# Reordering the attention heads of the second block: scores, transposes and weighing moved against the projections, the weight split moved behind the exponentials

## The chip, the cores and the metric

The kernel runs on one core of a Trainium2 chip. The metric is the device time of one execution in microseconds (us). An engine is one of the core's five: TensorE (PE; its weight loads are PEld), VectorE (DVE), ScalarE (ACT), GpSimd (POOL), and SyncE (SP), which here only issues the loads of weights.

## The reference

Two blocks of two layers each, over one sequence of 512 tokens of width 1024. The change is in the second block, in the part of a layer that computes differential attention (four heads of two 64-wide query/key maps each), and in the stick-breaking attention behind it. Cut to what matters:

```python
for layer in range(DEPTH):
    h = rms_norm_2(x, mix_norm_g[layer])
    proj = h @ w_in[layer]                       # 1024 -> 2720 columns
    da_q, da_k, da_v, sb_q, sb_k, sb_v, c_q, c_kv, k_r = jnp.split(proj, pts, axis=-1)
    y_a = diff_attention(da_q, da_k, da_v, ...)
    y_b = stick_breaking(sb_q, sb_k, sb_v, ...)
    y_c = latent_attention(c_q, c_kv, k_r, ...)
    x = x + concatenate([y_a, y_b, y_c]) @ w_out[layer]
    ...                                          # memory attention, feed-forward

# diff_attention, per head:
#   q, k = rms_norm(q), rms_norm(k)              over each 64-wide half
#   s_m  = q_m @ k_m.T * 64**-0.5 + bias_m       m = 0, 1 (chunk-causal mask)
#   a    = softmax(s_0) - lambda * softmax(s_1)
#   o    = rms_norm(a @ v)
```

All values are float32. The kernel writes each matmul operand as a rounded high part plus the remainder (`_hi`, `_lo`) and computes three products (hi x hi, lo x hi, hi x lo).

## The kernel before, in words

Everything is written out by hand in one program per engine, with counting semaphores between them; the order in the source is the order on each queue. The layer is a loop body that runs twice. Activations lie feature-major: 128 features on the partitions, 512 tokens in the free dimension.

A **unit** is one projection tile: 1024 x 128 weights, times the normed input, into one of two PSUM banks (`acc`). On PE it is 8 chunks (k = 0 to 7) of three matmuls, 128 x 512 each (lines 674, 675, 680; the last is 677). A unit's weights arrive raw by DMA, ACT makes the high part (`split`, L1306), POOL the remainder in two halves (L642, L643), always two units ahead of use.

Per head h PE computes three units: queries of head h+1, keys of head h+1, values of head h+1 (after the last head: the three of the stick-breaking attention). Between the chunks of these units it does the attention of the heads, at places given by the `before(k)` callbacks: the **scores** of head h (`da_scores`, L980 and L982, four query tiles of 128 rows and growing width, two maps each), the **turns** (`da_turn`, L701 and L703: the weights a are transposed, 10 tiles of 128 x 128 per head), **weighing** the values (`weigh_values`), the turn of the value tile (`turn_v`, into the bank `misc`) and the **sums** (`head_sum`, L948: a matmul with ones that sums squares over the partitions, also into `misc`). `take_misc` makes PE wait until the last reader of `misc` has taken its content.

The other engines follow the same list. DVE adds the bias to each score tile and takes the row maximum (`da_scores`, L2361 and L2363), takes the units out of PSUM (`take_unit`, `values`, L2320), forms a from the two softmaxes (`da_weights`, L2369 to L2377), scales by the norms (`head_norm`, L2305: queries, keys, and `da_output` for the output of the head before), and makes remainders (L2335, L2310). ACT exponentiates the score tiles (`da_exps`, L1661, eight per head), squares (`head_square`, L1590), and turns a sum of squares into 1/sqrt by Ln and Exp (`head_rstd`, L1598 and L1600), evicts the turned tiles (`turned_a`, L1637), and makes high parts. `output` on ACT is: `split` for two units ahead (unless `new=False`), then wait until the unit is computed and taken.

In the stick-breaking part behind (`sb_heads`), `keys` is the last step of the first pair of heads; after it come the norms and the high and low parts of the first two rows of c_q (`cq`, `cqh`, `cql`), which are used much later, in the latent attention.

## Time and profile before

| | us |
|---|---|
| median of 3 runs (3458.43 to 3461.69) | 3458.94 |
| the profiled execution, its own time | 3458.43 |
| its span | 3456.4 |
| PE busy | 3132.0 (91%) |
| DVE busy | 1612.6 (47%) |
| ACT busy | 1455.5 (42%) |
| POOL busy | 789.9 (23%) |

Busy time is the time in which at least one instruction of the engine ran. Matmuls overlap in the array, so that a row's duration (0.40 us) is longer than the distance between two starts (0.23 us); what PE loses is read from the starts. In a row of windows stand the stretch, its length, and for each engine (PE, PEld, DVE, ACT, POOL; PE alone where the engine was chosen) the busy time and the count, then the granted clock of TensorE as a share of 2.4 GHz, the DMA share and GB/s. A bracket at a timeline row's end is the time for which the engine stood idle before it and the instruction that released it.

### The profile page before, as it was taken

The numbers are of one execution on the slowest core, as the hardware profiler recorded it, in microseconds if no ns is written. First come the engines' busy times: TensorE is split into PE (matmuls) and PEld (weight loads), VectorE is DVE, ScalarE is ACT, GpSimd is POOL, SyncE is SP. The second block draws the span as 40 slices with busy tenths as digits, with TensorE's granted clock in tenths as the row PEclk, the third lists the DMA queues.
The fourth block names the chain that finished last, engine by engine and source line by source line (L and its number), as shares of the span: only waits on it lengthen the run. The fifth ranks groups of instructions, "written<-read, shape, count | busy, mean of one in ns | idle before, by whom it ended". The sixth has DMA issues, their size and how long they took to land.

```text
span 3456.4 us, 43795 instructions
## 1 busy us (share of the span) xinstructions
PE 3132.0 (91%) x13571; PEld 2451.1 (71%) x13571; DVE 1612.6 (47%) x2425; ACT 1455.5 (42%) x2128; POOL 789.9 (23%) x528
## 2 busy tenths in 40 slices
PE   6999999799998937999969988799998997889998
PEld 4788887588885725888857756578886774668886
DVE  4544454475574545655747445431124735341113
ACT  3333333443344544433436565443334665443233
POOL 1333332100001311000013221144443221224443
PEclk8999999899998968999989989799999998879999
DMA  8322221233331312333322111123333210213332
GB/s 195 110 79 80 77 75 55 61 104 102 94 92 42 92 31 57 102 104 92 97 62 69 54 57 31 37 84 94 94 95 99 62 57 25 61 37 98 91 97 73
DMA packets 486165, 269.41 MB, mean 78 GB/s; under 512 B 9418, under 2 KB 477458, under 8 KB 485620
## 3 DMA queue, kind: packets, MB, share of 16 engines
q1 hardware_dynamic: 479236, 255.85, 26.3%
q10 hardware_dynamic: 6768, 11.62, 1.0%
q8 instruction: 77, 1.26, 0.2%
q14 instruction: 84, 0.69, 0.1%
HBM read 264.12 MB, written 12.21 MB: 80 GB/s over the span
## 4 chain that ended last, share of the span: by engine, by line
issue 53%; PE 30%; POOL 11%; DVE 3%; ACT 2%; SPq 1%; DMA 0%; POOLq 0%; ACTq 0%; DVEq 0%
PE acc L674 9%; PE acc L675 9%; PE acc L680 7%; POOL s_w_lo L643 5%; POOL s_w_lo L642 4%; POOL s_w_lo L625 2%; PE acc L677 1%; PE wide L701 1%; PE misc L675 0%; PE misc L674 0%; PE misc L680 0%; PE wide L674 0%; DMA s_raw<-attn_w_qkv 0%; SPq L520 0%; DVE s_sc L2129 0%
## 5 line engine op out<-in xcount | busy, mean ns | idle before, releaser
L674 PE MATMUL acc<-s_h_hi,s_w_hi 128*128 128x512 f32 (+1 forms) x2128 | 880.8, 414 | 117.3 <-DVE s_h_lo L2289 37.6
L675 PE MATMUL acc<-s_h_lo,s_w_hi 128*128 128x512 f32 (+1 forms) x2128 | 845.0, 397 | 0.0
L680 PE MATMUL acc<-s_h_hi,s_w_lo 128*128 128x512 f32 (+1 forms) x1862 | 740.2, 398 | 0.0
L642 POOL TENSOR_TENSOR s_w_lo<-s_raw,s_w_hi 128x512 fp32r<-128x512 f32 x208 | 268.4, 1291 | 1575.5 <-ACT s_w_hi L1306 1573.7
L674 PEld LDWEIGHTS acc<-s_h_hi,s_w_hi 128*128 128x128 f32 x2128 | 407.7, 192 | 241.0 <-issue 78.3
L1306 ACT ACTIVATE s_w_hi<-s_raw 128x1024 fp32r<-128x1024 f32 x388 | 411.6, 1061 | 389.7 <-DVE s_x L2664 210.9
L625 POOL TENSOR_TENSOR s_w_lo<-s_raw,s_w_hi 128x1024 fp32r<-128x1024 f32 x108 | 258.6, 2395 | 1062.4 <-ACT s_w_hi L1306 1059.2
L675 PEld LDWEIGHTS acc<-s_h_lo,s_w_hi 128*128 128x128 f32 x2128 | 409.2, 192 | 95.9 <-issue 10.6
L680 PEld LDWEIGHTS acc<-s_h_hi,s_w_lo 128*128 128x128 f32 x1862 | 357.2, 192 | 83.6
L674 PE MATMUL acc<-s_hid_hi,s_w_hi 128*128 128x512 f32 x752 | 297.4, 395 | 0.0
L675 PE MATMUL acc<-s_hid_lo,s_w_hi 128*128 128x512 f32 x752 | 297.3, 395 | 0.0
L643 POOL TENSOR_TENSOR s_w_lo<-s_raw,s_w_hi 128x512 fp32r<-128x512 f32 x208 | 271.3, 1304 | 0.0
L680 PE MATMUL acc<-s_hid_hi,s_w_lo 128*128 128x512 f32 x658 | 260.0, 395 | 0.0
L674 PE MATMUL acc<-s_h_hi,s_w_hi_f 128*128 128x512 f32 x432 | 177.1, 410 | 20.9 <-DVE s_h_lo L1982 11.1
L675 PE MATMUL acc<-s_h_lo,s_w_hi_f 128*128 128x512 f32 x432 | 173.5, 402 | 0.0
L2654 DVE SCALAR_TENSOR_TENSOR s_u<-acc,s_rstd 128x512 f32<-128x512 f32 x64 | 44.3, 692 | 271.2 <-PE acc L677 260.4
L674 PEld LDWEIGHTS acc<-s_hid_hi,s_w_hi 128*128 128x128 f32 x752 | 141.5, 188 | 33.9
L675 PEld LDWEIGHTS acc<-s_hid_lo,s_w_hi 128*128 128x128 f32 x752 | 141.5, 188 | 33.7
L680 PE MATMUL acc<-s_h_hi,s_w_lo_f 128*128 128x512 f32 x378 | 151.8, 402 | 0.0
L1486 ACT ACTIVATE s_cv<-s_up,s_cols 128x512 f32<-128x512 f32 x96 | 78.5, 818 | 164.2 <-DVE s_up L2197 160.5
L2207 DVE SCALAR_TENSOR_TENSOR s_cv<-s_up,s_cols,s_cv 128x512 f32<-128x512 f32 x192 | 144.1, 750 | 6.1
L680 PEld LDWEIGHTS acc<-s_hid_hi,s_w_lo 128*128 128x128 f32 x658 | 123.8, 188 | 29.6
(402 smaller groups left out, 4841.6 us busy)
## 6 DMA issues: line engine op xcount, KB each, us to landing
s_raw<-w_ff SPq DMA_DIRECT2D x128, 512.0 KB, 4.0
s_raw<-ffn_w_up SPq DMA_DIRECT2D x96, 512.0 KB, 3.9
s_raw<-attn_w_qkv SPq DMA_DIRECT2D x72, 512.0 KB, 3.7
s_raw<-ffn_w_down SPq DMA_DIRECT2D x48, 512.0 KB, 3.9
s_raw<-w_in SPq DMA_DIRECT2D x44, 512.0 KB, 4.0
s_raw<-lru_w_in SPq DMA_DIRECT2D x16, 512.0 KB, 4.0
s_raw<-w_out SPq DMA_DIRECT2D x16, 512.0 KB, 3.8
s_raw<-attn_w_o SPq DMA_DIRECT2D x8, 512.0 KB, 3.9
```

Of the source, the lines that this page charges most:

```text
L625: pool.tensor_tensor(w_lo_of[w][:], raw_b[s][:], w_hi_of[w][:].bitcast(F32), ALU.subtract).then_inc(sems["unit_ready"], 1)
L642: pool.tensor_tensor(w_lo_b[s][:, 0:h, :], raw_b[s][:, 0:h, :], w_hi_b[s][:, 0:h, :].bitcast(F32), ALU.subtract)
L643: pool.tensor_tensor(w_lo_b[s][:, h:, :], raw_b[s][:, h:, :], w_hi_b[s][:, h:, :].bitcast(F32), ALU.subtract).then_inc(sems["unit_ready"], 1)
L674: mm(out, ahi, bhi, start=start, stop=False, **kw)
L675: mm(out, ahi, blo, start=False, stop=False, **kw)
L677: mm(out, alo, bhi, start=False, stop=stop, **kw).then_inc(sems[sem], 1)
L680: mm(out, alo, bhi, start=False, stop=stop, **kw)
L701: nc.tensor.transpose(*args)
L1306: fn((w_hi_a if count.ring == "A" else w_hi_b)[w][:], raw_b[s][:], ACT.Copy).then_inc(sems["hi_split"], 1)
L1486: fn(cv[:, s, :], up[:, s, 2:2 + S], ACT.Identity, bias=cols[:, bass.ds(b * KC + v, 1)], scale=cols[:, bass.ds(b * KC + w, 1)]).then_inc(s ...
L2207: stt(cv[:, s, :], up[:, s, tap:tap + S], cols[:, bass.ds(b * KC + w, 1)], cv[:, s, :], ALU.mult, ALU.add).then_inc(sems[sem], 1)
L2654: stt(u2[:, n % 2, :], o[:], 0.0, rstd[:], ALU.max, ALU.mult).then_inc(sems["acc_freed"], 1)
```

## The change

No instruction is added or removed; the order changes on PE, ACT and DVE.

1. **PE.** The turns of head h move from chunk 2 of the query unit of the next round to chunk 6 of the value unit of the same round. Weighing and the value turn move two chunks forward (6 and 7 to 4 and 5). The first two score tiles move from the key unit's chunk 1 to the query unit's chunk 6, the last two from chunk 4 to chunk 3, the output's sum from 2 to 1, and the sum for the keys in the value unit from chunk 5 to chunk 4.
2. **ACT.** Each `split` moves from ahead of the exponentials to behind them. The Ln and Exp for the previous head's output move from ahead of exponentials 5 to 8 to between the 6th and the 7th. The Ln and Exp for the next queries move behind the square of the next keys.
3. **DVE.** The norm of the previous head's output moves from behind all eight score tiles to between the 6th and the 7th.
4. **Stick-breaking part.** Norms, high and low parts of `cq` move into `keys`, ahead of ACT's square of the head output (`od`) and of DVE's copy of it out of PSUM.

```diff
                 def beside_queries(h):
                     def before(k):
-                        if k == 2 and h > 0:
-                            for q in range(TT):
-                                da_turn(q)
-                        if k == 6 and h > 0:
+                        if k == 4 and h > 0:
                             weigh_values()
-                        if k == 7:
+                        if k == 5:
                             turn_v(1)
-                    return before
-
-                def beside_keys(h):
-                    def before(k):
-                        if k == 1:
+                        if k == 6:
                             pe.wait_ge(sems["hn_lo"], count("hn_lo", 2))
                             for q in range(0, 2):
                                 da_scores(q)
-                        if k == 2 and h > 0:
+                    return before
+
+                def beside_keys(h):
+                    def before(k):
+                        if k == 1 and h > 0:
                             head_sum(ONES, first=1)
-                        if k == 4:
+                        if k == 3:
                             for q in range(2, 4):
                                 da_scores(q)
                     return before
...
-                        if k == 5 and h < HEADS_2 - 1:
+                        if k == 4 and h < HEADS_2 - 1:
                             head_sum(HALVES, first=1)
+                        if k == 6:
+                            for q in range(TT):
+                                da_turn(q)
...
                 def beside_common(k):
-                    if k == 2:
-                        for q in range(TT):
-                            da_turn(q)
-                    if k == 6:
+                    if k == 4:
                         weigh_values()
-                    if k == 7:
+                    if k == 5:
                         turn_v(1)
...
+                def da_rstds():
+                    head_rstd(SUB)
+                    head_rstd(SUB, dst=kr[:])
...
                 for h in range(HEADS_2):
-                    split()
                     da_exps(range(0, 4))
-                    output(new=False)
+                    output()
                     if h < HEADS_2 - 1:
                         head_square(tn[:, 0, :])
+                    da_exps(range(4, 6))
                     if h > 0:
                         norm_output(P)
-                    split()
-                    da_exps(range(4, 8))
-                    if h < HEADS_2 - 1:
-                        head_rstd(SUB)
-                    output(new=False)
+                    da_exps(range(6, 8))
+                    output()
                     if h < HEADS_2 - 1:
                         head_square(tn[:, 1, :], part=1)
-                        head_rstd(SUB, dst=kr[:])
-                    split()
+                        da_rstds()
                     for q in range(TT):
                         turned_a(q)
...
                 def keys():
                     output()
                     sb_hi(1)
                     head_rstd(2 * P)
+                    head_hi(cqh[:, 0, :], cq[:, 0, :])
+                    head_hi(cqh[:, 1, :], cq[:, 1, :])
                 sb_heads(last_norm, rows_squares, queries, keys)
                 square_output()
                 head_square(cq[:, 2, :], part=1)
-                head_hi(cqh[:, 0, :], cq[:, 0, :])
-                head_hi(cqh[:, 1, :], cq[:, 1, :])
...
-                    da_scores(h, range(4, 8))
+                    da_scores(h, range(4, 6))
                     if h > 0:
                         da_output(h - 1)
+                    da_scores(h, range(6, 8))
                     take_unit(1)
                     da_weights()
...
                 def keys():
                     take_unit(1)
                     sb_lo(1)
+                    head_norm([(cq[:, n, :], cq[:, n, :], n) for n in range(2)], "mla_cq_norm_g_2", 2)
+                    for n in range(2):
+                        head_lo(cql[:, n, :], cq[:, n, :], cqh[:, n, :])
```

ACT, second head, from the square of the next queries (`s_sq<-s_tn`) on; register instructions between the rows are left out. Before:

```order
L1590 ACTIVATE s_sq<-s_tn 128x512
L1598 ACTIVATE s_rs<-misc,s_eps 128x512
L1600 ACTIVATE s_rs<-s_rs 128x512
L1306 ACTIVATE s_w_hi<-s_raw 128x1024
L1661 ACTIVATE s_sd,s_sm<-s_sd,s_sm 128x384
...
L1661 ACTIVATE s_sd,s_sm<-s_sd,s_sm 128x512
L1598 ACTIVATE s_rs<-misc,s_eps 128x512
L1600 ACTIVATE s_rs<-s_rs 128x512
L1590 ACTIVATE s_sq<-s_tn 128x512
L1598 ACTIVATE s_kr<-misc,s_eps 128x512
```

The same piece of the change, where line numbers differ by the lines that the diff takes and adds ahead of them:

```order
L1587 ACTIVATE s_sq<-s_tn 128x512
L1662 ACTIVATE s_sd,s_sm<-s_sd,s_sm 128x384
...
L1595 ACTIVATE s_rs<-misc,s_eps 128x512
L1597 ACTIVATE s_rs<-s_rs 128x512
L1662 ACTIVATE s_sd,s_sm<-s_sd,s_sm 128x512
...
L1303 ACTIVATE s_w_hi<-s_raw 128x1024
L1587 ACTIVATE s_sq<-s_tn 128x512
L1595 ACTIVATE s_rs<-misc,s_eps 128x512
L1597 ACTIVATE s_rs<-s_rs 128x512
L1595 ACTIVATE s_kr<-misc,s_eps 128x512
```

The output's Ln and Exp (first `s_rs` pair) now stand behind two exponentials, the split (`s_w_hi`) behind all, and the queries' Ln and Exp behind the keys' square.

DVE at the same place, from the 6th score tile on, before:

```order
L2361 TENSOR_TENSOR s_sd<-wide,s_bd 128x384
L2363 TENSOR_REDUCE s_sm<-s_sd 128x1
L2361 TENSOR_TENSOR s_sd<-wide,s_bd 128x512
...
L2305 SCALAR_TENSOR_TENSOR s_yo<-s_od,s_cols,s_rs 128x512
L2320 TENSOR_TENSOR s_tn<-acc,s_rstd 128x512
L2369 RECIPROCAL s_sm<-s_sm 128x8
```

and in the change:

```order
L2356 TENSOR_TENSOR s_sd<-wide,s_bd 128x384
L2358 TENSOR_REDUCE s_sm<-s_sd 128x1
L2300 SCALAR_TENSOR_TENSOR s_yo<-s_od,s_cols,s_rs 128x512
L2356 TENSOR_TENSOR s_sd<-wide,s_bd 128x512
...
L2315 TENSOR_TENSOR s_tn<-acc,s_rstd 128x512
L2364 RECIPROCAL s_sm<-s_sm 128x8
```

The norm of the output (`s_yo`), which reads ACT's `s_rs`, now stands ahead of the two widest tiles.

DVE at the end of the first pair of stick-breaking heads, before:

```order
L2310 SCALAR_TENSOR_TENSOR s_kl<-s_tn,s_kh 128x512
L2341 COPY s_od<-acc 64x512
L2305 SCALAR_TENSOR_TENSOR s_cq<-s_cq,s_cols,s_rs 128x512
...
L2310 SCALAR_TENSOR_TENSOR s_cql<-s_cq,s_cqh 128x512
...
L2305 SCALAR_TENSOR_TENSOR s_yo<-s_od,s_cols,s_rs 128x512
```

and in the change:

```order
L2305 SCALAR_TENSOR_TENSOR s_kl<-s_tn,s_kh 128x512
L2300 SCALAR_TENSOR_TENSOR s_cq<-s_cq,s_cols,s_rs 128x512
...
L2305 SCALAR_TENSOR_TENSOR s_cql<-s_cq,s_cqh 128x512
...
L2336 COPY s_od<-acc 64x512
L2300 SCALAR_TENSOR_TENSOR s_yo<-s_od,s_cols,s_rs 128x512
```

The copy of the head output stands behind four instructions that stood behind it.

## Rows read from the trace of the kernel before

**Rows 1.** The page: busy time, share of the span, instructions of each engine.
```profile
PE 3132.0 (91%) x13571; PEld 2451.1 (71%) x13571; DVE 1612.6 (47%) x2425; ACT 1455.5 (42%) x2128; POOL 789.9 (23%) x528
```

**Rows 2.** Windows, four heads: us, busy us (count) per engine, granted clock, DMA.
```profile
1820.27:1929.78 109.51, 106.48 (x536) 81.33 (x534) 81.61 (x160) 67.35 (x133) 33.29 (x26) 1.00 0.24 64
```

**Rows 3.** Waits, 1820 to 1930: total us, times, longest.
```profile
PE misc L948 <- ACT s_sq L1590: 1.9, 3, 1.0
PE wide L701 <- DVE s_sd L2377: 1.1, 2, 0.6
```

**Rows 4.** Timeline of PE, second to fourth head: start us, duration.
```profile
1842.34 0.40 PE L674 MATMUL acc<-s_h_hi,s_w_hi 128*128 128x512 f32 x1
...
1856.16 0.44 PE L980 MATMUL wide<-s_kh,s_qh 64*128 64x384 f32 x2
...
1864.57 0.40 PE L680 MATMUL acc<-s_h_hi,s_w_lo 128*128 128x512 f32 x1
1865.96 1.12 PE L948 MATMUL misc<-s_sq,s_square 128*128 128x512 f32 x2 [0.99 <-ACT s_sq L1590]
...
1869.01 0.40 PE L674 MATMUL acc<-s_h_hi,s_w_hi 128*128 128x512 f32 x1
...
1870.41 0.27 PE L703 MATMUL wide<-s_square,s_sd 128*128 128x128 f32 x1
...
1871.42 0.48 PE L674 MATMUL acc<-s_h_hi,s_w_hi 128*128 128x512 f32 x1
...
1895.37 0.40 PE L674 MATMUL acc<-s_h_hi,s_w_hi 128*128 128x512 f32 x1
...
1929.78 0.32 PE L1052 MATMUL wide<-s_qh,s_kh 64*128 64x128 f32 x1
```

**Rows 5.** Timeline of DVE, second head: score tiles 5, 6, 8, a step of the difference.
```profile
1856.99 0.56 DVE L2361 TENSOR_TENSOR s_sd<-wide,s_bd 128x384 f32<-128x384 f32 x1 [0.95 <-PE wide L982]
...
1858.63 0.55 DVE L2363 TENSOR_REDUCE s_sm<-s_sd 128x1 f32<-128x384 f32 x1
...
1861.14 0.69 DVE L2363 TENSOR_REDUCE s_sm<-s_sd 128x1 f32<-128x512 f32 x1
...
1865.27 0.48 DVE L2377 SCALAR_TENSOR_TENSOR s_sd<-s_sd,s_sm 128x256 f32<-128x256 f32 x1
```

**Rows 6.** Timeline of ACT, second head: exponential, Ln, and the square of the keys.
```profile
1858.63 1.06 ACT L1306 ACTIVATE s_w_hi<-s_raw 128x1024 fp32r<-128x1024 f32 x1 [0.18 <-ACT s_rs L1600]
...
1863.66 0.69 ACT L1598 ACTIVATE s_rs<-misc,s_eps 128x512 f32<-128x512 f32 x1 [0.48 <-ACT s_sd L1661]
...
1865.20 0.63 ACT L1590 ACTIVATE s_sq<-s_tn 128x512 f32<-128x512 f32 x1 [0.18 <-ACT s_rs L1600]
```

**Rows 7.** Timeline of DVE, fourth head: reciprocal and first, last delayed steps.
```profile
1916.49 0.20 DVE L2369 RECIPROCAL s_sm<-s_sm 128x8 f32<-128x8 f32 x1
...
1917.97 1.40 DVE L2377 SCALAR_TENSOR_TENSOR s_sd<-s_sd,s_sm 128x256 f32<-128x256 f32 x1
...
1921.83 0.75 DVE L2377 SCALAR_TENSOR_TENSOR s_sd<-s_sd,s_sm 128x512 f32<-128x512 f32 x1
```

**Rows 8.** Timeline of POOL at the same place.
```profile
1917.70 1.39 POOL L642 TENSOR_TENSOR s_w_lo<-s_raw,s_w_hi 128x512 fp32r<-128x512 f32 x1 [2.99 <-ACT s_w_hi L1306]
```

**Rows 9.** PE after an idle time elsewhere: timeline row, then window row.
```profile
1116.47 0.50 PE L674 MATMUL acc<-s_h_hi,s_w_hi 128*128 128x512 f32 x1 [3.86 <-POOL s_w_lo L625]
...
1118.00:1120.00 2.00, 2.00 (x6) 0.50 0.77 228
```

**Rows 10.** Timeline of DVE and PE, end of the first stick-breaking pair.
```profile
1981.14 0.69 DVE L2341 COPY s_od<-acc 64x512 f32<-64x512 f32 x1
1982.10 0.75 DVE L2305 SCALAR_TENSOR_TENSOR s_cq<-s_cq,s_cols,s_rs 128x512 f32<-128x512 f32 x1 [0.27 <-DVE s_od L2341]
...
1984.01 1.52 DVE L2310 SCALAR_TENSOR_TENSOR s_cql<-s_cq,s_cqh 128x512 fp32r<-128x512 f32 x2 [0.25 <-ACT s_cqh L1605]
1984.13 1.02 PE L948 MATMUL misc<-s_sq,s_square 128*128 128x512 f32 x2
```

More of the change, by code:

```diff
@@ L993, in before @@
                     def before(k):
-                        if k == 2 and h > 0:
-                            for q in range(TT):
-                                da_turn(q)
-                        if k == 6 and h > 0:
+                        if k == 4 and h > 0:
                             weigh_values()
-                        if k == 7:
+                        if k == 5:
                             turn_v(1)
+                        if k == 6:
+                            pe.wait_ge(sems["hn_lo"], count("hn_lo", 2))
+                            for q in range(0, 2):
+                                da_scores(q)
                     return before
@@ L1004, in before @@
                     def before(k):
-                        if k == 1:
-                            pe.wait_ge(sems["hn_lo"], count("hn_lo", 2))
-                            for q in range(0, 2):
-                                da_scores(q)
-                        if k == 2 and h > 0:
+                        if k == 1 and h > 0:
                             head_sum(ONES, first=1)
-                        if k == 4:
+                        if k == 3:
                             for q in range(2, 4):
@@ L1684, in layer @@
                 for h in range(HEADS_2):
-                    split()
                     da_exps(range(0, 4))
-                    output(new=False)
+                    output()
                     if h < HEADS_2 - 1:
                         head_square(tn[:, 0, :])
+                    da_exps(range(4, 6))
                     if h > 0:
                         norm_output(P)
-                    split()
-                    da_exps(range(4, 8))
-                    if h < HEADS_2 - 1:
-                        head_rstd(SUB)
-                    output(new=False)
+                    da_exps(range(6, 8))
+                    output()
                     if h < HEADS_2 - 1:
                         head_square(tn[:, 1, :], part=1)
-                        head_rstd(SUB, dst=kr[:])
-                    split()
+                        da_rstds()
                     for q in range(TT):
@@ L1707, in layer @@
                         sb_hi(1)
-                    output(new=False)
+                    output()
                     last_head()
@@ L2478, in keys @@
                     sb_lo(1)
+                    head_norm([(cq[:, n, :], cq[:, n, :], n) for n in range(2)], "mla_cq_norm_g_2", 2)
+                    for n in range(2):
+                        head_lo(cql[:, n, :], cq[:, n, :], cqh[:, n, :])
                 fill_cq(0)
                 sb_heads(last_norm, lambda: fill_cq(2), queries, keys)
-                head_norm([(cq[:, n, :], cq[:, n, :], n) for n in range(2)], "mla_cq_norm_g_2", 2)
-                for n in range(2):
-                    head_lo(cql[:, n, :], cq[:, n, :], cqh[:, n, :])
                 head_norm([(yo[:, 4, :], od[:], 0)], "sb_out_g_2")
```

## The prediction, written before the changed kernel ran

> **What bounds the kernel now.** Read the page first: PE is busy for 91% of the span, DVE, ACT and POOL for 47, 42 and 23% [rows 1]. So the question is where PE waits in the part that changes. The windows show the four heads: 109.51 us in a layer, PE busy for 106.48 of them at full clock [rows 2]; the second layer's program is the same, so every term counts twice. The list of waits says what the rest is: three waits of the sum for the keys (L948) for ACT's square, 1.9 us, and two of the turns (L701) for DVE's weighted difference, 1.1 us [rows 3]. That is all that the change can win here, 3.0 us a layer, 6.1 us in all. Then the timeline of the second head: its round lasts from 1842.34 to 1869.01, 26.67 us, the third one's to 1895.37, 26.36 us, and from there to the end of the common unit pass 34.41 us [rows 4]. In the second head the wide scores start on PE at 1856.16, the matmul ahead of the second sum at 1864.57, and the sum at 1865.96 [rows 4]. A matmul starts 0.23 us behind the last, so PE was there at 1864.80: 8.64 us behind the scores, and it waited 1.16.
>
> **PE's own work in the change.** It does the same instructions. From the wide scores to the second sum there are nine chunks, the scores and one sum in both orders (4+1+4 before, 5+1+3 after), so PE arrives again 8.64 us behind the scores. The scores start earlier in the round: the turns (1870.41 to 1871.42, with the slower start behind them 1.1 us) and one chunk of three matmuls (0.7) no longer stand ahead: 13.82 - 1.8 = 12.0 us. PE gains nothing by that alone, it has the turns at the round's end instead.
>
> **The chain to the second sum, times from the start of the wide scores.** DVE's fifth tile starts at 0.83, the sixth one's maximum is there at 1859.18, so 3.0 [rows 5]. ACT's sixth exponential takes 0.9 (its 0.62 and the accumulator's 0.19, and a gap): 3.9. Now come the output's Ln and Exp, which had run ahead of the fifth: from 1863.66 to the square's start at 1865.20 pass 1.54, less the gap of 0.18: 1.36 [rows 6], so 5.3. Only now can DVE, idle since 3.0, norm the output: 0.86, of which 0.75 is such an instruction [rows 10] and the rest the gap to the next: 6.15. Its last two tiles take 2.7 (maxima at 1859.18 and 1861.83) [rows 5]: 8.9. The eighth exponential ends at 9.75. The split, now behind it, takes 0.18 + 1.06, the square 0.18 + 0.63 [rows 6]: 11.8. And the sum may not overwrite the bank before ACT has taken the queries' sum out of it: that Ln was ahead of the square and is behind it now, 0.18 + 0.69 + 0.1: the sum starts at 12.8. PE has been there at 8.64: **a wait of 4.15 us in place of 1.16**.
>
> **The turns behind it.** From the sum to the round's end were three chunks, 3.05 us (1865.96 to 1869.01) [rows 4]; two of them bring PE to 15.15, where the turns now stand. DVE starts the reciprocal at 9.8. The fourth head shows what follows if POOL's remainder of the weights falls beside it: POOL from 1917.70 [rows 8], a step that reads SBUF alone 1.40 long [rows 7] where the same takes 0.48 in the second head [rows 5], and the one behind it likewise. From the reciprocal at 1916.49 to the last tile at 1922.58 pass 6.09 us [rows 7]; two steps of 0.98 us less or so would make it 4.1. There the split started right behind the last exponential, as it now does in every head. So the last tile is ready at 15.9, is turned by 16.3, and two chunks (1.5) end the round at 17.8. 12.0 + 17.8 = 29.8: **+3.1 for the second head, +3.4 for the third**. In the fourth there is no sum, but the turns wait for the same 15.9 and the value unit ends at 29.8 too; the common unit, eight chunks (5.6), weighing and value turn (2.4), brings 37.8 against 34.41: **+3.4**. The first head norms no output: its last reciprocal stands at 6.6, its sum at 9.5 against an arrival at 8.64, its turns end at 13.1, the round at 23.8 against 22.07 (1820.27 to 1842.34) [rows 2, 4]: **+1.7**. That holds the moved turns of 1.1, which the last term gives back. A layer: 1.7 + 3.1 + 3.4 + 3.4 = 11.6.
>
> On POOL and DVE the row came first; the Trainium skill's page "SBUF — State Buffer" (section "SBUF: two separate sides") says that they take a shared port pair by an exclusive lock, whole instructions long, when the DVE instruction has two SBUF inputs or runs in a two-port mode. The trace agrees (1.40 for 0.48 us). By the rule the later norms and remainders are held as well, which stand beside PE's next query unit and change no term.
>
> **The weights.** With the split behind the exponentials, unit remainders are ready later: the one from the key output at 11.0 + 2.7 for a unit that starts at 17.8, the one from the query output 2 us ahead of its unit. I cost that at nothing; if the cover went, PE would wait for POOL at a unit's start, up to 1 us a head. Scores in the query unit need the remainders of queries and keys, ready 4 us ahead. Weighing needs the last turned tile, ready about 1 us ahead.
>
> **The stick-breaking part.** DVE copies the head output at 1981.14; in the change the two norms and two remainders of `cq` stand ahead. From the first norm, 1982.10, to the end of the remainders, 1985.53, are 3.4 us [rows 10]; they can start with the Exp's end, 1981.87, so the copy starts at 1985.4, its square ends at 1986.7, and PE's sum, which did not wait at 1984.13 [rows 10], starts 2.6 late. Behind it follow the output's Ln and Exp, the split and the softplus of the next pair, which wait for that unit: nothing absorbs it. **+2.6 a layer** (0 if the next pair had slack, 4.2, the delay of the copy, at most). Taking the high parts off the later stretch saves ACT an idle stretch only.
>
> **The clock.** A wait of 4 us is not only itself. Where PE idled 3.86 us at 1116, it went on at full speed for 0.8 us, and then the granted clock was 0.50, which is 1.2 GHz of 2.4 [rows 9]; eight matmuls started 0.43 instead of 0.23 us apart, 1.6 us lost. The heads had no such wait, and 1.00 [rows 2]. The change makes three a layer (second, third, fourth head). Lost time there is PE's own, since turns, chunks and the next query unit follow: 3 x 1.6 = 4.8. Bounds: 0 and, if each stretch lasts twice as long, 9.6.
>
> The page "TensorE: Matmul & The Clock Gate" (section "What's actually happening") of the skill says that a gate halves the array's clock by how busy PE has been; the trace agrees. Without the rule the sum would be 9.6 us less.
>
> **Sum.** 11.6 + 2.6 + 4.8 = 19.0 a layer, 38 in two. The profiled execution took 3458.43 us (span 3456.4), 0.5 under the median of 3458.94, so 3458.4 + 38 = **3496 us**.
>
> **Rivals.**
> - *The clock stays up.* For it: the first layer's idle second sum (1 us) left it at 1.00 [rows 2]. Against: [rows 9] is the nearest row in length. 3496 - 9.6 = 3487.
> - *POOL's remainder misses the weighted difference.* The last tile is then ready 1.95 sooner. The second and third head gain 0.8 each (PE reaches the turns at 15.15), the fourth 1.95, the first 1.2: 4.7 a layer, 9.5 in all: 3487. Against it: the order of exponential, split, reciprocal is that of the fourth head [rows 7, 8].
> - *The waits deepen.* If each slow stretch lasts twice as long, or also slows the scores behind the stick-breaking sum: +9.6, 3506.
> - *Faster.* The one mechanism: ACT finishes the output's Ln and Exp while DVE is still at the narrow tiles, so the square is there when PE comes. Then the waits of 3.0 us a layer go, 3458.4 - 6.1 = 3452. It decides at 8.64: the chain must be 4.15 us shorter than I add it up. Of the 12.8, DVE's idle time is 2.3, the split 1.24 and the Ln 0.97; all three would have to be wrong.
> - *It does not do what it says.* The order on the engines shows that it does; what may fail is that waits hidden elsewhere make it neutral, at most the 2.6 of the stick-breaking part and half the heads: 3470.
>
> **Numbers.** Forecast with all three terms 0.57, clock up 0.15, POOL missed 0.08, deeper 0.10, near 3470 0.05, faster 0.03, no change 0.02. A measurement of this kernel tells 0.2% (7 us) from no change. The range leaves out 3470 and below, and most of the deepest: 3481 to 3505. Faster 0.03, within 0.2% 0.03, slower 0.94.
>
> **What would show it.** In the changed profile: in the heads DVE idle 2.3 us ahead of its output norm (L2300), waiting for ACT's Exp; PE idle about 4 us ahead of the second sum in the value units of heads two and three, waiting for ACT's Ln; two steps of 1.4 us in every weighted difference; PE waits ahead of the turns of the fourth head of some 5 us; the four heads at 121 us at full clock, 126 with the slow stretches; granted clock 0.50 behind each wait; PE idle 2.6 us ahead of the sum that was at 1984. I am wrong if the second sum waits under 2 us, or if the copy of the stick-breaking output doesn't wait for `cql`.

## The result and the profile after

| kernel | median | profiled execution | span | ratio to before |
|---|---|---|---|---|
| before | 3459.64 us | 3458.43 | 3456.4 | 1 |
| changed | 3499.76 us (4 runs, 3499.07 to 3505.51) | 3504.37 | 3502.3 | 1.0119, 95% interval 1.0101 to 1.0137 |

The changed kernel is 40 us slower; forecast were 38 (3496, range 3481 to 3505). The median of before moved between 3457.2 and 3461.1 us from one set of runs to the next, so the experiments below are compared by their ratio to before, measured beside them; a ratio of 0.001 is 3.46 us.

The page of the changed kernel, busy time of each engine. It answers to [rows 1]:

```profile
PE 3149.0 (90%) x13571; PEld 2461.7 (70%) x13571; DVE 1627.4 (46%) x2425; ACT 1455.4 (42%) x2128; POOL 793.9 (23%) x528
```

Same instructions, but PE's busy time grew by 17 us. That is a first sign: not all of the loss is waiting, some is PE's own work done slower.

The windows of the changed kernel: the four heads and the common unit of the first layer, the stick-breaking stretch behind them, and the four heads of the second layer (us, busy us and count of each engine, granted clock, DMA share, GB/s):

```profile
1821.94:1949.54 127.60, 113.72 (x536) 85.43 (x534) 89.75 (x161) 68.36 (x135) 35.04 (x26) 0.93 0.20 55
...
1949.54:2009.44 59.90, 57.27 (x234) 41.03 (x233) 18.40 (x31) 33.23 (x60) 13.62 (x11) 0.95 0.16 45
2668.82:2796.08 127.26, 113.39 (x536) 85.13 (x534) 89.89 (x161) 68.34 (x135) 35.04 (x26) 0.93 0.21 55
```

The heads took 109.51 at clock 1.00 [rows 2]; now 127.60: 18.1 us more, of which PE's busy time is 7.2 and its idle time 10.9. The second layer gives the same, 17.8 (127.26 against 109.49). For the stick-breaking stretch the same windows of the kernel before:

```profile
1929.78:1987.17 57.39, 57.39 (x233) 41.26 (x232) 18.63 (x32) 33.61 (x61) 12.64 (x10) 0.94 0.17 46
2756.14:2810.45 54.31, 54.31 (x233) 39.63 (x232) 19.41 (x32) 33.64 (x62) 12.63 (x10) 1.00 0.18 49
```

Its undisturbed length is 54.31; the 57.39 of the first layer holds a slow stretch of its own, at clock 0.94. In the changed kernel it is 59.90 in both layers: 2.5 and 5.6 more. Sum: 18.1 + 17.8 + 2.5 + 5.6 = 44.0 of the 45.9 by which the two spans differ. Of the rest 1.7 is already there where the heads begin (1821.94 against 1820.27), ahead of anything that the change touches. The change is found where it was made, and nothing comes back later.

The list of PE's waits in the first layer's heads (us in total, times, longest), against 1.9 and 1.1 in [rows 3]:

```profile
PE misc L948 <- ACT s_rs L1595: 9.0, 3, 4.4
PE wide L701 <- DVE s_sd L2372: 3.1, 4, 1.3
PE wide L703 <- DVE s_sd L2372: 1.8, 1, 1.8
```

PE's timeline in the second head (start, duration; in brackets the idle time ahead and its releaser), the place of [rows 4]:

```profile
1858.02 0.44 PE L980 MATMUL wide<-s_kh,s_qh 64*128 64x384 f32 x2
...
1866.41 0.40 PE L680 MATMUL acc<-s_h_hi,s_w_lo 128*128 128x512 f32 x1
1871.20 2.08 PE L948 MATMUL misc<-s_sq,s_square 128*128 128x512 f32 x2 [4.39 <-ACT s_rs L1595]
1872.29 1.42 PE L674 MATMUL acc<-s_h_hi,s_w_hi 128*128 128x512 f32 x1
1873.51 0.63 PE L675 MATMUL acc<-s_h_lo,s_w_hi 128*128 128x512 f32 x1
1873.93 0.63 PE L680 MATMUL acc<-s_h_hi,s_w_lo 128*128 128x512 f32 x1
...
1875.64 0.41 PE L703 MATMUL wide<-s_square,s_sd 128*128 128x128 f32 x1
```

PE could start the sum 8.6 us behind the wide scores and starts it 13.18 behind them. That is 4.6 from start to start, the measure of the prediction (which forecast 4.15, and took 1.16 for before); the trace, which counts from the modelled end of the last matmul, calls it 4.39 (0.99 before). Waits below are given as the trace counts them. The matmuls behind it then start 0.42 us apart and not 0.23. The window of just these says why (the 0.50 behind POOL's count is the granted clock):

```profile
1872.29:1875.64 3.35, 3.35 (x9) 2.15 (x7) 3.08 (x5) 1.32 (x2) 0.00 (x0) 0.50 0.59 156
```

DVE in the same head, the place of [rows 5]:

```profile
1860.49 0.55 DVE L2358 TENSOR_REDUCE s_sm<-s_sd 128x1 f32<-128x384 f32 x1
1863.48 0.75 DVE L2300 SCALAR_TENSOR_TENSOR s_yo<-s_od,s_cols,s_rs 128x512 f32<-128x512 f32 x1 [2.44 <-ACT s_rs L1597]
...
1867.97 0.20 DVE L2364 RECIPROCAL s_sm<-s_sm 128x8 f32<-128x8 f32 x1 [0.28 <-ACT s_sd L1662]
...
1869.44 1.37 DVE L2372 SCALAR_TENSOR_TENSOR s_sd<-s_sd,s_sm 128x256 f32<-128x256 f32 x1
1870.74 1.42 DVE L2370 TENSOR_SCALAR s_sd<-s_sd,s_sm 128x384 f32<-128x384 f32 x1
...
1873.24 0.75 DVE L2372 SCALAR_TENSOR_TENSOR s_sd<-s_sd,s_sm 128x512 f32<-128x512 f32 x1
```

and ACT and POOL there, the places of [rows 6] and, for POOL, [rows 8]:

```profile
1868.12 1.06 ACT L1303 ACTIVATE s_w_hi<-s_raw 128x1024 fp32r<-128x1024 f32 x1 [0.18 <-ACT s_sd L1662]
1869.65 0.63 ACT L1587 ACTIVATE s_sq<-s_tn 128x512 f32<-128x512 f32 x1 [0.48 <-ACT s_w_hi L1303]
1870.46 0.69 ACT L1595 ACTIVATE s_rs<-misc,s_eps 128x512 f32<-128x512 f32 x1 [0.18 <-ACT s_sq L1587]
```

```profile
1869.25 1.28 POOL L642 TENSOR_TENSOR s_w_lo<-s_raw,s_w_hi 128x512 fp32r<-128x512 f32 x1 [8.82 <-ACT s_w_hi L1303]
```

Read them as one chain. DVE is through with its sixth tile and stands idle 2.44 us for ACT's Exp (L1597) of the output; the last two tiles come only behind that norm, then the last exponential, the split (1868.12), the square, the queries' Ln (ends 1871.15), and the sum starts at 1871.20. Beside it POOL's remainder, set off by that split, starts at 1869.25, and two DVE steps take 1.37 and 1.42 where one took 0.48 [rows 5].

The fourth head has no second sum. There PE waits for DVE's tiles one by one:

```profile
1933.16 0.33 PE L703 MATMUL wide<-s_square,s_sd 128*128 128x128 f32 x1 [1.76 <-DVE s_sd L2372]
1934.83 0.47 PE L701 MATMUL wide<-s_square,s_sd 128*128 128x128 f32 x1 [1.34 <-DVE s_sd L2372]
...
1936.82 0.69 PE L701 MATMUL wide<-s_square,s_sd 128*128 128x128 f32 x2 [1.31 <-DVE s_sd L2372]
```

With a last 0.29 that is 4.7 us. And the end of the first stick-breaking pair, the place of [rows 10], on DVE and then on PE:

```profile
2000.47 1.52 DVE L2305 SCALAR_TENSOR_TENSOR s_cql<-s_cq,s_cqh 128x512 fp32r<-128x512 f32 x2
2002.11 0.69 DVE L2336 COPY s_od<-acc 64x512 f32<-64x512 f32 x1
```

```profile
2003.60 2.07 PE L948 MATMUL misc<-s_sq,s_square 128*128 128x512 f32 x2 [2.63 <-ACT s_sq L1587]
2004.68 1.42 PE L674 MATMUL acc<-s_h_hi,s_w_hi 128*128 128x512 f32 x1
```

The copy stands behind `cql`, the sum waits 2.63, and the clock falls here too: the sum takes 1.08 us to the next matmul's start where it takes 0.56 at full speed, and the last section shows the window.

### The profile page after: what moved, and what is told of

It reads as the page before. It is cut to its first block, busy times and chain, and to the rows that moved or that the text cites. A ratio compares the mean times of both kernels' runs of the same rounds, so it can differ in the third digit from the quotient of the medians.

```text
span 3502.3 us, 43795 instructions
## 1 busy us (share of the span) xinstructions
PE 3149.0 (90%) x13571; PEld 2461.7 (70%) x13571; DVE 1627.4 (46%) x2425; ACT 1455.4 (42%) x2128; POOL 793.9 (23%) x528
## 4 chain that ended last, share of the span: by engine, by line
issue 53%; PE 29%; POOL 11%; DVE 3%; ACT 2%; SPq 1%; POOLq 0%; DMA 0%; DVEq 0%; ACTq 0%
PE acc L674 9%; PE acc L675 8%; PE acc L680 7%; POOL s_w_lo L643 5%; POOL s_w_lo L642 4%; POOL s_w_lo L625 2%; PE acc L677 1%; PE wide L701 1%; PE misc L675 0%; PE misc L674 0%; PE wide L674 0%; PE misc L680 0%; DMA s_raw<-attn_w_qkv 0%; SPq L520 0%; PE wide L675 0%
```

## The experiments

The theory after this: three pieces add up (PE's order, ACT's and DVE's order in the heads, the stick-breaking move), the second carries most, and a quarter or so of the whole loss is PE's clock behind the waits. The rivals: PE's new order is what costs; the clock falls for another reason; the collision of POOL and DVE counts for nothing. "Heads" below is the first layer's window over the four heads and the common unit, 109.51 before and 127.60 changed.

### The three pieces, each alone on the kernel before

**pe_only**: PE's hunks of the diff, nothing else.

> The kernel before, with only PE's part of the change (turns in the value unit, scores, weighing and sums at their new places); ACT and DVE keep their old order. My theory (PE's new order costs little, the order on ACT and DVE costs the rest): the second sum still waits about 1.2 us, the first three heads' last tiles are ready before PE comes to the turns, the fourth's are up to 1.7 late, and the first head's round keeps the moved turns, which the common unit gives back: +1 to +2 us a layer, 3463 us (3458 to 3468). Rival (the turns moved ahead in time are what PE waits for): the last tile is late in every head by what norm_back showed and more, 3 us a layer and head, 3475 us or more.

Measured 3467.12 us, ratio 1.0019 (1.0010 to 1.0028): +6.6 us. Heads of the first layer:

```profile
1821.25:1932.26 111.01, 106.77 (x535) 81.27 (x533) 81.30 (x161) 68.35 (x135) 33.33 (x26) 1.00 0.23 63
```

1.50 more, as expected, at full clock. The second layer's heads took 112.56, 3.1 more, as the clock fell once there, at 2749.8, behind the turns' waits; the expectation had no term for that. The second sums wait 0.3 to 0.6; the fourth head's turns 3.0 in place of 1.1. The rival's 3475 is out: by itself PE's new order costs little.

**act_only**: ACT's and DVE's hunks in the heads.

> The kernel before, with only ACT's and DVE's part of the change in the heads (splits, the output's norm, the queries' Ln); PE and the stick-breaking part keep the old order. My theory (this order carries the cost): the second sum waits about 4.1 us in heads 2 and 3, 0.6 more in head 1, and the turns of head 4 about 3.2 more, 10.2 a layer, and three slow stretches of some 1.6: 15 a layer, 3490 us (3481 to 3496). Rival (only with PE's new order do the waits reach this size, because its turns stand closer behind the last tile): under 3475 us.

Measured 3487.09 us, ratio 1.0083 (1.0070 to 1.0097): +29. The heads take 125.71, 16.2 more, at clock 0.95; the second sum waits 4.38 and 4.00. So this order makes the long waits without PE's new order. In the fourth head the expectation was nearly right in size (3.2) by luck. It is not the turns that are late there, but the weights of the common unit:

```profile
1933.12 0.49 PE L674 MATMUL acc<-s_h_hi,s_w_hi 128*128 128x512 f32 x1 [3.84 <-POOL s_w_lo L643]
```

PE, with its turns still in the common unit, comes to that unit early, and the remainder that follows the late split is not there.

**sb_only**: the move of the `cq` norms ahead of the copy, by the last hunks of the diff.

> The kernel before, with only the move of the cq norms, remainders and high parts ahead of the stick-breaking output's copy. My theory: PE's sum waits 2.6 us a layer where it waited for nothing, 5.2 us in all, and a stretch of granted clock 0.50 may follow, up to 2.2 us each: 3465 to 3470 us. Rival (the delay is made up in the next pair, whose scores wait for other things): 3460 us.

Measured 3470.84 us, ratio 1.0028 (1.0017 to 1.0039): +9.8, at the upper end of what was named (2.6 + 2.2 a layer). The wait is 2.63, the stretch 58.79 in place of 54.31, heads unchanged (109.51).

The three ratios add up to 1.0130, the whole change measured 1.0119 (1.0101 to 1.0137). Of that sum the order on ACT and DVE is two thirds, the stick-breaking move a fifth, PE's order the rest. That the sum fits so well has some luck in it: the 3.84 of act_only is absent in the changed kernel, whose fourth head waits for the turns in its place.

### One piece taken back from the changed kernel

**norm_back**: the output's norm at its old place.

```diff
-                    da_exps(range(4, 6))
                     if h > 0:
                         norm_output(P)
-                    da_exps(range(6, 8))
+                    da_exps(range(4, 8))
...
-                    da_scores(h, range(4, 6))
+                    da_scores(h, range(4, 8))
                     if h > 0:
                         da_output(h - 1)
-                    da_scores(h, range(6, 8))
```

> The changed kernel, with only the output's norm put back in the heads: ACT's Ln and Exp ahead of exponentials 4 to 7, DVE's norm of the previous output behind score tiles 4 to 7. My theory (the wait for DVE's norm sits in the chain to the second sum, and the stall lowers the clock): counted from the wide scores, tiles end at 5.7, the last exponential at 6.6, split and square at 8.65, the Ln that frees the bank at 9.6, against PE's arrival at 8.64: the sum waits 1.0 us in place of 4.0 to 4.4, the round of heads 2 to 4 is 3.15 us shorter, and the three stretches of granted clock 0.50 (1.6 each) go. 9.45 + 4.8 = 14.3 a layer, 28.5 in all: 3471 us (3466 to 3478). Rival A (only DVE's idle time of 2.3 goes, the clock does not follow the waits): 6.9 a layer, 3486 us. Rival B (the new place of the turns on PE is what costs): the sum's wait goes, and the turns wait instead, 3495 us or more.

Measured 3480.62 us, ratio 1.0058 (1.0044 to 1.0072): 0.0061 less than the changed kernel, 21 us. The heads of the first and of the second layer, and the second sum:

```profile
1820.47:1934.65 114.18, 107.77 (x536) 81.17 (x534) 88.92 (x161) 68.39 (x135) 36.67 (x26) 1.00 0.23 60
```

```profile
1866.32 1.12 PE L948 MATMUL misc<-s_sq,s_square 128*128 128x512 f32 x2 [1.00 <-ACT s_rs L1595]
```

The wait is 1.00, as expected; in the first layer the clock is 1.00 and the heads are 13.4 shorter (14.3 expected). In the second they take 115.80 and are 11.5 shorter, because the clock fell once, at 2759.2, behind the waits of the fourth head's turns. Together that is 24.9, the timed difference 21, with some 8 us of uncertainty. The total came out above the 3466 to 3478 named; part of that are the turns' waits and the clock behind them, which were not in the sum. Rival A wanted 6.9 a layer. Rival B wanted the turns' waits in place of the sum's; they wait 3.9 in all, where the changed kernel's had 4.9, so nothing moved there.

**split_back**: the three splits ahead of the exponentials and the turned copies.

```diff
+                    split()
                     da_exps(range(0, 4))
-                    output()
+                    output(new=False)
...
+                    split()
                     da_exps(range(4, 6))
...
+                    split()
                     for q in range(TT):
                         turned_a(q)
```

> The changed kernel, with only the three splits of a head put back ahead of the exponentials and the turned copies on ACT. My theory: the split's 1.24 us leave the chain to the sum (waits of heads 2 and 3 go from 4.4 and 4.0 to 3.1 and 2.8), and POOL's remainder no longer falls beside the weighted difference (steps of 0.48 in place of 1.40 us), so the last tile is 1.95 earlier; heads 2 to 4 end 1.95 earlier, head 1 1.2: 7.05 a layer, 3486 us, if a wait of 3 us still lowers the clock; if it does not, 3476. Rival (POOL's remainder is not what makes the two steps long): the last tile stays, the turns wait in place of the sum, 3500 us.

Measured 3491.42 us, ratio 1.0096 (1.0080 to 1.0111): 8 us less than the changed kernel, about 8 either way, so that the reading rests on the windows. The first layer's heads take 121.08, 6.5 less (7.05 expected), but not where expected: 1.3, 2.2 and 2.9 in the first three, 0.1 in the fourth. The second layer's take 123.22, 4.0 less. DVE's steps in the second head, and the same pair in the fourth:

```profile
1867.97 0.48 DVE L2375 SCALAR_TENSOR_TENSOR s_sd<-s_sd,s_sm 128x256 f32<-128x256 f32 x1
1868.37 0.41 DVE L2373 TENSOR_SCALAR s_sd<-s_sd,s_sm 128x384 f32<-128x384 f32 x1
...
1926.77 1.50 DVE L2375 SCALAR_TENSOR_TENSOR s_sd<-s_sd,s_sm 128x256 f32<-128x256 f32 x1
1928.19 1.42 DVE L2373 TENSOR_SCALAR s_sd<-s_sd,s_sm 128x384 f32<-128x384 f32 x1
```

```profile
1926.73 1.26 POOL L642 TENSOR_TENSOR s_w_lo<-s_raw,s_w_hi 128x512 fp32r<-128x512 f32 x1 [8.04 <-ACT s_w_hi L1303]
```

In the first three heads nothing of POOL lies beside the difference and the steps take 0.48 and 0.41. In the fourth ACT has no squares to do between the last exponential and the third split, so POOL starts at 1926.73, beside the first of the two steps. The collision is shown by its presence and its absence in one program. I had overlooked that the fourth head is the one place where undoing the split changes nothing. (The Trainium skill, page "SBUF — State Buffer", section "SBUF: two separate sides", tells of the lock between the two engines; these rows agree.)

**ln_back**: the queries' Ln and Exp behind the last exponential, ahead of the keys' square.

```diff
+                    if h < HEADS_2 - 1:
+                        head_rstd(SUB)
                     output()
                     if h < HEADS_2 - 1:
                         head_square(tn[:, 1, :], part=1)
-                        da_rstds()
+                        head_rstd(SUB, dst=kr[:])
```

> The changed kernel, with only the queries' Ln and Exp put back ahead of the keys' output and square on ACT. My theory: the sum starts 0.4 us later in heads 2 and 3 (Ln and Exp of 1.36 in the chain in place of one Ln of 0.97), but the turns behind it wait for the last tile anyway, which stays: no difference, 3500 us (3497 to 3504). Rival (the bank held until the Ln is what makes the sum wait): 0.97 less in the chain, 2 heads x 2 layers x 1 us, 3496 us or less.

Measured 3510.83 us, ratio 1.0144 (1.0129 to 1.0160): slower still, by 0.0025, where I expected nothing (the two intervals overlap). The trace is clearer: the sums wait 1.56, 4.84 and 4.70 in place of 0.66, 4.39 and 3.96, and the heads take 130.46, 2.9 more. The shift in the second and third head was right or nearly (0.4 and 0.7), the claim that the turns hide it was wrong: in the changed kernel's second head the last tile is done at 1873.99 and PE comes to the turns at 1875.64, so nothing waits there that could hide it. In the first head the wait grew by 0.9, which I had not counted. The waits explain 2.1 a layer; the rounds grew by 0.5, 0.0, 2.0 and 0.3, and the difference lies in where the clock was low, as these windows stand at 0.92 and 0.93. Taken by the waits, this reorder is the one piece of the change that helps.

**sb_back**: `cq` behind the copy and the square again.

> The changed kernel, with only the norms, remainders and high parts of cq put back behind the stick-breaking output's copy and square. My theory as corrected by the trace (a wait of 2.63 us a layer, and a stretch at half clock behind it that costs 2.2): 4.8 a layer, 3500 - 9.7 = 3490 us. Rival A (the slow stretch there has another cause and stays): 5.3 less, 3494.5 us. Rival B (the copy's delay is hidden by the next pair's scores): 3500 us.

Measured 3495.50 us, ratio 1.0098 (1.0083 to 1.0114): 7 us less, but about 8 either way, so that the times decide between none of the three. The windows do, for this execution: the stretch is back at 54.33 us in the first layer and 54.32 in the second, at clock 1.00, and PE does not wait in it. From 59.90 that is 5.6 a layer, more than the wait of 2.63. Rival B is out, and so is rival A's slow stretch that stays. Outside these windows and the heads its span is 4 us longer, where the edit changes nothing, which is why the total shows less.

### The clock by itself

**fill**: matmuls of no use into PE's waits. The diff shows the part in the heads; the nine matmuls ahead of the common unit's sum, and the helper's branch for them, are left out of it.

```diff
+                def filler(n):
+                    s, o = count.slot(), bank[count.bank()]
+                    for j in range(n):
+                        mm(o[:], w_lo_b[s][:, j % KC, :], h_lo[:, j % KC, :], start=False, stop=False)
...
                         if k == 4 and h < HEADS_2 - 1:
+                            filler((0, 16, 14)[h])
                             head_sum(HALVES, first=1)
                         if k == 6:
                             for q in range(TT):
+                                filler((6, 4, 4, 0)[q] if h == HEADS_2 - 1 else 0)
                                 da_turn(q)
```

> The changed kernel, with matmuls of no use where PE waits: 16 and 14 ahead of the second sum of heads 2 and 3 (of waits of 4.39 and 3.96 us), 6, 4 and 4 ahead of the first three turns of head 4, 9 ahead of the stick-breaking sum (of 2.63). In the heads they add the product of the two remainders to the unit, which is nothing at this precision; in the stick-breaking part they write a bank that the next unit starts anew. At 0.23 us each they fit into the waits. My theory (PE's idle time is what lowers the clock): sums and turns start when they did, the granted clock stays 1.00 in heads 1 to 4 and behind the stick-breaking sum, and the stretches' cost goes: 2.1 + 1.6 + 1.9 + 2.7 = 8.3 a layer by the changed kernel's timeline, 3500 - 16.6 = 3483 us. Rival A (the clock falls for another reason, such as the order's load on the chip): 3500 us, clock 0.50 as before. Rival B (the added matmuls delay the work behind them): over 3500 us.

Measured 3498.14 us, ratio 1.0114 (1.0098 to 1.0129). The forecast of 3483 failed, and by the time alone rival A looks right. The heads say otherwise:

```profile
1821.97:1943.95 121.98, 117.56 (x579) 89.21 (x578) 89.25 (x161) 68.39 (x135) 36.11 (x26) 1.00 0.21 56
```

```profile
1866.64 3.90 PE L982 MATMUL acc<-s_h_lo,s_w_lo 128*128 128x512 f32 x16
1871.21 1.12 PE L948 MATMUL misc<-s_sq,s_square 128*128 128x512 f32 x2 [0.67 <-ACT s_rs L1610]
1871.77 0.80 PE L674 MATMUL acc<-s_h_hi,s_w_hi 128*128 128x512 f32 x1
1872.40 0.39 PE L675 MATMUL acc<-s_h_lo,s_w_hi 128*128 128x512 f32 x1
```

Counted from the start of the span, the sum starts 0.01 us from where it did. All of the 16 fit into its wait, and the clock is 1.00: 127.60 - 121.98 = 5.6 us a layer is the clock. The second layer gives 5.3 (127.26 - 121.97). It is no accident of one execution: with the filler the heads of both layers stayed at 1.00 in fill and in fill2, four of four, and without it the clock fell three times in each layer's heads in the changed kernel, sb_back and ln_back, six of six. (The Trainium skill, page "TensorE: Matmul & The Clock Gate", section "What's actually happening", has the gate follow how busy PE has been; this test agrees, as the chain is unchanged and only PE's idle time is gone.) Where did the gain go? The stick-breaking filler was at the wrong sum: the wait of 2.63 remained, and nine matmuls stood ahead of the common unit, which ended 1.2 us later for them. In the second layer the clock fell at 2839.3, right behind the wait that I had not filled, and again at 2846.1, 8 us behind it with no wait of that size between.

**fill2**: the filler of ten at the right sum, none in the common unit.

> As fill, with the stick-breaking filler where the wait of 2.63 us is: 10 matmuls of no use ahead of the sum in the value unit of the second stick-breaking pair, and none ahead of the common unit, where fill had put 9 of them into no wait (they moved all behind them by 2.1 us a layer). My theory: 2 x 2.1 less than fill, and the granted clock stays 1.00 behind the sum, 0 to 2.2 a layer: 3492 us (3487 to 3496). Rival (stretches that go here come back later in the layer): 3498 us as fill.

Measured 3487.60 us, ratio 1.0085 (1.0071 to 1.0099): 0.0034 under the changed kernel, 12 us (about 8 either way; 16.6 was the sum). The heads take 121.99 at clock 1.00, the stick-breaking stretch 57.21, in both layers; by these windows it is 16.3 less than the changed kernel. So the clock is some 12 of the 40 us by the times, and 16 of the 46 by the profiled executions; the rest is waits and moved work.

### Better than both

**before_ln**: the kernel before with the one piece that helps.

> The kernel before, with one piece of the change: the queries' Ln and Exp behind the square of the keys on ACT. My theory, from ln_back (the first head's sum waited 1.56 with the Ln ahead and 0.66 with it behind; the second's 4.84 and 4.40): the sum of the keys waits about 0.4 to 0.9 us less in each of three heads, up to 1.9 us a layer: 3456 to 3459 us, at the edge of what can be told. Rival (the queries' norm on DVE becomes late and the scores wait for its remainder): 3463 us or more.

Measured 3454.80 us beside 3461.07, ratio 0.9985 (0.9976 to 0.9994), 5 us less where up to 3.8 were expected. The sums wait 0.6 us in place of 1.9, and the heads are 1.6 a layer shorter:

```profile
1822.65:1930.55 107.90, 106.22 (x536) 81.40 (x534) 81.56 (x160) 67.36 (x133) 33.60 (x26) 1.00 0.24 64
```

**best**: that, and the fourth head's third split behind its turned copies.

```diff
+                    if h < HEADS_2 - 1:
+                        split()
                     for q in range(TT):
                         turned_a(q)
+                    if h == HEADS_2 - 1:
+                        split()
```

> The kernel before, with the queries' Ln and Exp behind the square of the keys (as before_ln), and in the fourth head ACT's split behind the turned copies, so that POOL's remainder does not fall beside the weighted difference on DVE. My theory: before_ln's 3455 less 1.1 us a layer (the turns' waits of 0.48 and 0.64 go; two DVE steps of 0.48 in place of 1.40): 3452 us (3448 to 3456). Rival (the later split makes a unit's weights late for PE): 3457 us or more.

Measured 3452.30 us beside 3457.15, ratio 0.9984 (0.9975 to 0.9993):

```profile
1817.19:1923.54 106.35, 105.79 (x535) 81.44 (x533) 80.97 (x160) 67.33 (x133) 33.79 (x26) 1.00 0.23 60
```

The turns' waits are gone and the heads are another 1.6 a layer shorter, which the time can't tell from before_ln. It is faster than both kernels: than before by 5 us (2 to 9). Some 0.6 us of wait a layer are left in the heads.

**pe_best**: the same with PE's new order.

> As best, with PE's new order. My theory: the second sum's waits of 0.3 to 0.6 go with the Ln, and of the fourth head's turn waits (0.77, 1.56, 0.64) all but about 1 us: no difference from best, 3452 to 3458 us. Rival (PE's new order is better once ACT's order suits it): under 3449 us.

Measured 3454.59 us, ratio 0.9992 (0.9983 to 1.0001), heads 107.39: no gain from PE's order. Its turns wait 1.2 in the fourth head, as it comes to them sooner.

## Why the prediction was right, and where its sizes were off

The prediction was right in its mechanism (the chain to the second sum, the collision, the copy behind `cql`, the clock behind the waits) and in its size. That 38 came so near to 40 is in part luck, as the last items say.

- **What bounds the heads.** PE did, at 109.51 us with 3.0 of waits. The bound on what could be won, 3.0 a layer, was a little low: the best order found takes 106.35, 3.2 less, with 0.6 of waits left.
- **The chain to the second sum.** Counted from the wide scores at 1858.02 of the second head: norm at 5.46 (forecast 5.3), reciprocal at 9.95 (9.8), sum at 13.18 (12.8), wait 4.56 from start to start (4.15), last tile ready 15.97 (15.9). The missing 0.4 is the square, which waited 0.48 and not 0.18 behind the split, and 0.15 on DVE. PE itself came to the turns 0.4 later than forecast (15.5 in fill, in place of 15.15). norm_back shows that the norm's place makes 3.4 of the 4.39, ln_back that the Ln behind the square lowers it.
- **The rounds without the clock**, which fill shows apart:

| round | before | forecast | fill | changed |
|---|---|---|---|---|
| first head | 22.07 | 23.8 | 23.98 | 23.99 |
| second | 26.67 | 29.8 | 30.10 | 32.70 |
| third | 26.36 | 29.8 | 29.94 | 31.30 |
| fourth and common unit | 34.41 | 37.8 | 37.96 | 39.61 |

  12.5 us a layer in place of 11.6.
- **POOL beside the weighted difference.** Forecast for every head, found in every head (1.37 or 1.38 and 1.42 or 1.43). The rival that it misses is out.
- **The clock in the heads.** 4.8 a layer forecast, 5.6 measured by fill: 2.6, 1.4 and 1.7 in heads two to four, where 1.6 each was taken from the one fall at 1116. The rival of a clock that stays up is out; deeper waits did not come either.
- **The stick-breaking part.** 2.6 forecast, wait 2.63, and 57.21 - 54.31 = 2.9 with all that hangs on it at full clock (fill2, norm_back). Here is the term that was mis-sized: the prediction counted three falls of the clock a layer, all in the heads, though a fourth wait of 2.6 us stood in the same sum; a slow stretch behind it appears only in the rival of deeper waits. Where the clock fell it added up to 2.7 more.
- **Sum.** Forecast 11.6 + 4.8 + 2.6 = 19.0 a layer. In the changed kernel's second layer: 17.8 + 5.6 = 23.4; in the first 18.1 + 2.5 = 20.6, as the kernel before lost 3.1 there to a slow stretch of its own. The profiled execution of the changed kernel lies 4.6 above its median and that of before 1.2 below, so the medians differ by 40, not 46. The forecast of 38 was low by the stick-breaking clock, by 0.9 of waits and by 0.8 of the heads' clock a layer, and the medians are kind to it.
- **The weights.** Cost nothing, right for this change: PE waits for no remainder in the heads. act_only shows how near it was, with 3.84 in one place once PE comes earlier.

## What to carry to other kernels

Do not place a step that waits for another engine between two steps of a chain that a third engine needs: the norm is 0.75 us of DVE, but its place cost 3.3 to 3.4 us in each of two sums. Price an added wait on TensorE twice, the wait itself and the matmuls behind it at the lower granted clock (here 1.4 to 2.6 us behind waits of 4 us or three shorter ones in a row, 0 to 2.7 behind one of 2.6), and do that for every wait of a few microseconds, not only for the longest. Matmuls of no use in the gap tell the two apart. Judge a piece of 5 us by its window in the trace, as its time alone is within the noise. And see what a split sets off on the next engine: an instruction moved by a microsecond on ACT decided whether POOL and DVE met.

## What the runs showed of the hardware that was not expected

The same wait, to 0.01 us, does not always lower the clock alike. PE's wait for the stick-breaking sum was 2.62 or 2.63 in every kernel that had the move; what followed it was not the same. The stretch from the sum to the end of its unit in the changed kernel, and then in both layers of norm_back:

```profile
2003.60:2009.44 5.84, 5.84 (x12) 3.48 (x12) 0.75 (x1) 2.91 (x4) 0.99 (x1) 0.50 0.00 1
```

```profile
1988.71:1991.86 3.15, 3.15 (x12) 1.99 (x12) 0.41 (x1) 2.23 (x4) 0.00 (x0) 1.00 0.00 0
...
2823.94:2828.69 4.75, 4.75 (x11) 2.83 (x11) 0.75 (x1) 2.91 (x4) 0.00 (x0) 0.64 0.00 2
```

The same twelve matmuls (a record can be missing) took 5.84 us at 0.50, 3.15 at 1.00 and, in the other layer of one and the same execution, 4.75 at 0.64; sb_only and ln_back lay there too (4.74 at 0.64 and 4.73 at 0.65). In split_back the wait of 3.16 of the second sum was followed by five slow projection matmuls and slow turns, the 2.72 of the third by none.

Nor does every fall stand behind a long wait. The kernel before had two in its stick-breaking parts with no wait of over 0.7 us in the 60 us ahead: at 1933.04, 3.3 us into the stick-breaking scores that start where the heads' window ends, and at 2830.74.

```profile
1933.04:1939.86 6.82, 6.82 (x14) 3.90 (x14) 2.15 (x5) 5.96 (x12) 1.30 (x2) 0.50 0.28 78
```

PE was busy through all of it, and through the 10 us ahead of it at 1.00; the change and its four waits are not needed for a fall. This is the slow stretch of its own that the windows above showed for the first layer. So the clock's part of a wait of 2 to 3 us is a matter of a few us a layer either way. That this is why pieces of 5 us came out unevenly in the times while their windows fitted is likely, but not shown. What decides it in a given execution was not tried.
